# Expert stage of a hybrid decoder layer: weights stationary and tokens moving, in blocks of three tiles with four widths

## What is computed

```python
def routed_experts(h, w_router, b_router, w_up, b_up, w_down, b_down):
    ht = h.reshape(T, D)                                   # 2048 x 1024
    logits = (ht @ w_router + b_router).astype(jnp.float32)
    top_vals, top_idx = lax.top_k(logits, TOP_K)           # 4 of 32
    gate = jax.nn.softmax(top_vals, axis=-1)
    ...
    xs = ht[tok]                                           # 8192 rows, sorted by expert
    hid = lax.ragged_dot(xs, w_up, group_sizes) + b_up[e_sorted]       # 1024 -> 2048
    x_glu = jnp.minimum(hid[:, 0::2], SWIGLU_LIMIT)
    x_lin = jnp.clip(hid[:, 1::2], -SWIGLU_LIMIT, SWIGLU_LIMIT)
    act = x_glu * jax.nn.sigmoid(SWIGLU_ALPHA * x_glu) * (x_lin + 1.0)
    out = lax.ragged_dot(act, w_down, group_sizes) + b_down[e_sorted]  # 1024 -> 1024
    out = out * gate.reshape(-1)[order][:, None].astype(out.dtype)
    y = jnp.zeros_like(ht).at[tok].add(out)
```

## Time and profile before

| | |
|---|---|
| median of 3 runs | 5605.09 us (5603.74 to 5606.45) |
| profiled execution, its span | 5600.4 us |
| TensorE products busy | 5200.6 us, 93% |
| weight loads busy | 4371.7 us, 78% |
| VectorE, ScalarE, GpSimd busy | 49%, 35%, 12% |
| bytes moved by DMA | 810.15 MB, mean 145 GB/s |

### The profile page before, as it was taken

How to read it: one execution, slowest core, us unless ns; L and a number is a source line. 1 busy time by engine, 2 the same in 40 slices (tenths; PEclk the granted TensorE clock), 3 DMA queues, 4 the chain that set the end, 5 groups by cost and what they waited for, 6 DMA issues and landing times.

```text
span 5600.4 us, 88876 instructions
## 1 busy us (share of the span) xinstructions
PE 5200.6 (93%) x24906; PEld 4371.7 (78%) x24907; DVE 2741.4 (49%) x5402; ACT 1934.0 (35%) x3754; POOL 679.8 (12%) x767
## 2 busy tenths in 40 slices
PE   7999999998687799896999999999999999999996
PEld 6888888887566678685887878778877787888885
DVE  3000000000699744354566565775666666665564
ACT  3111111111355522222344444553444434343333
POOL 0000000000344300022011111111111111110110
PEclk7999999999799899897999999999999999999998
DMA  3221222122223243443467465764666656554556
GB/s 112 75 75 59 75 75 73 61 75 79 109 99 120 99 170 136 159 142 117 151 191 231 154 195 164 232 223 157 196 208 190 216 169 192 158 170 154 162 167 196
DMA packets 387048, 810.15 MB, mean 145 GB/s; under 512 B 62259, under 2 KB 113715, under 8 KB 380724
## 3 DMA queue, kind: packets, MB, share of 16 engines
q1 hardware_dynamic: 361188, 722.92, 37.5%
q0 software_dynamic: 25808, 86.59, 6.7%
HBM read 662.47 MB, written 155.26 MB: 146 GB/s over the span
## 4 chain that ended last, share of the span: by engine, by line
PE 46%; DMA 2%; DVE 2%; issue 1%; ACT 1%; DVEq 0%; SPq 0%; ACTq 0%; POOL 0%; POOLq 0%
PE e_acc L253 15%; PE e_acc L255 14%; PE e_acc L254 14%; DMA e_raw<-in_w_down 2%; PE e_xT L2049 1%; PE e_aT L2058 1%; DVE e_hid L2009 1%; ACT e_whi L1913 0%; DVE e_wlo L1974 0%; SPq L1806 0%; DVE e_alo L1984 0%; DVE e_glu L2011 0%; DMA e_xg<-h,e_rec_in 0%; ACT e_sg L1948 0%; DVE e_glu L2016 0%
## 5 line engine op out<-in xcount | busy, mean ns | idle before, releaser
L1974 DVE TENSOR_TENSOR e_wlo<-e_raw,e_whi 128x512 fp32r<-128x512 f32 x1544 | 953.1, 687 | 210.5 <-ACT e_whi L1913 207.7
L253 PE MATMUL e_acc<-e_whi,e_xhi 128*128 128x512 f32 x2592 | 1031.7, 398 | 17.8 <-issue 15.0
L255 PE MATMUL e_acc<-e_whi,e_xlo 128*128 128x512 f32 x2592 | 1012.9, 391 | 0.0
L254 PE MATMUL e_acc<-e_wlo,e_xhi 128*128 128x512 f32 x2592 | 1011.7, 390 | 0.0
L1913 ACT CAST e_whi<-e_raw 128x512 fp32r<-128x512 f32 x1544 | 830.9, 619 | 124.7 <-issue 84.7
L253 PE MATMUL p_acc<-p_hi,hT_hi 128*128 128x464 f32 x2048 | 765.8, 374 | 14.2 <-DVE p_lo L348 14.2
L255 PE MATMUL p_acc<-p_hi,hT_lo 128*128 128x464 f32 x2048 | 764.5, 373 | 0.0
L254 PE MATMUL p_acc<-p_lo,hT_hi 128*128 128x464 f32 x2048 | 761.7, 372 | 0.0
L348 DVE TENSOR_TENSOR p_lo<-p_raw,p_hi 128x464 fp32r<-128x464 f32 x128 | 79.5, 642 | 1078.9 <-ACT p_hi L318 1078.4
L253 PEld LDWEIGHTS e_acc<-e_whi,e_xhi 128*128 128x128 f32 x2592 | 487.2, 188 | 125.3 <-issue 27.9
L255 PEld LDWEIGHTS e_acc<-e_whi,e_xlo 128*128 128x128 f32 x2592 | 487.1, 188 | 103.1
(11 more groups left out here) (284 smaller groups left out, 6575.8 us busy)
## 6 DMA issues: line engine op xcount, KB each, us to landing
e_raw<-in_w_up SPq DMA_DIRECT2D x1032, 256.0 KB, 5.1
e_raw<-in_w_down SPq DMA_DIRECT2D x512, 256.0 KB, 6.7
z<-p_z SPq DMA_DIRECT2D x256, 232.0 KB, 2.0
e_bias<-in_b_up SPq DMA_DIRECT2D x129, 256.0 KB, 5.6
p_raw<-in_w_in SPq DMA_DIRECT2D x128, 232.0 KB, 2.8
b_gates<-z SPq DMA_DIRECT2D x16, 1536.0 KB, 7.1
oT<-x_oT SPq DMA_DIRECT2D x16, 1024.0 KB, 3.9
b_raw<-oT SPq DMA_DIRECT2D x16, 1024.0 KB, 9.4
```

Source lines behind the costliest of these rows:

```text
L253: pe.matmul(out, x_hi(k), w_hi(k), start=first, stop=False)
L254: pe.matmul(out, x_hi(k), w_lo(k), start=False, stop=False)
L255: mm = pe.matmul(out, x_lo(k), w_hi(k), start=False, stop=last)
L1974: dve.tensor_tensor(w_lo[s % 2][:, k, :], raw[:, k, :], w_hi[s % 2][:, k, :].bitcast(F32), ALU.subtract).then_inc(lo_made.sem, 1)
```

## The change

The roles of the operands are swapped in `run_experts`. A 128x128 piece of the weights is stationary, and the tokens of one block move: `x_hi` and `x_lo` (then `a_hi`, `a_lo`) hold channels on partitions and up to 384 tokens side by side. A block has at most three tiles. The planner writes into each row of the table which of four widths (256, 288, 320, 384 tokens) covers the tokens of the block, and TensorE branches to one of four copies of its code for the block, with that width in each product. A slice is now four fills (`j`), one for each 128 of its output columns, of 24 products each; the result has channels on partitions and tokens as columns.

The up columns are sorted while they are split: `pairs` reads every second column of `raw`, `banks` writes them side by side, so that a fill gives either clamped-half or linear-half channels. The bias is one number per partition now; all biases are loaded and turned once, at the start, and added as a column operand in the instruction that empties the bank. Activations need no transposes any more; outputs do (`turn_y`), before ScalarE gates them. VectorE now does both clamps, always over 384 columns; GpSimd keeps the indirect DMAs and two small copies. SyncE loads the next records after slice 2's weights instead of slice 1's.

```diff
-BLOCK_TILES = 4
+BLOCK_TILES = 3
+WIDTHS = (256, 288, 320, 384)
...
+            link(dve.tensor_copy(cntf[:], rkp[:, 0:E]))
...
+            link(dve.tensor_scalar(wide[:, 1:2], wide[:, 0:1], float(WIDTHS[0]), None, ALU.is_gt))
+            for w in WIDTHS[1:-1]:
+                link(dve.scalar_tensor_tensor(out=wide[:, 1:2], in0=wide[:, 0:1], scalar=float(w), in1=wide[:, 1:2],
+                                              op0=ALU.is_gt, op1=ALU.add))
...
+        def pairs(w, k, s):
+            if s >= UP:
+                return w[:, k, :]
+            return w[:, k, :].rearrange("p (h n a) -> p h a n", h=Q // 2, a=2)
+        def banks(w, k, s):
+            if s >= UP:
+                return w[:, k, :]
+            return w[:, k, :].rearrange("p (h a n) -> p h a n", h=Q // 2, a=2)
...
         def _(act):
-            def split(b, s, free):
+            def split(b, s, ks):
...
-                    act.copy(w_hi[s % 2][:, k, :], raw[:, k, :]).then_inc(hi_made.sem, 1)
+                    act.copy(banks(w_hi[s % 2], k, s), pairs(raw, k, s)).then_inc(hi_made.sem, 1)
...
+                for s in range(UP):
+                    for h in range(2):
+                        n = 2 * s + h
+                        act.wait_ge(taken.sem, taken.after(b, 2 * n + 1))
+                        act.activation(sg[n % 2][:], glu[n % 2][:], ACT.Sigmoid, scale=ALPHA).then_inc(sg_made.sem, 1)
+                        split(b, s + 1, range(4 * h, 4 * h + 4))
+                        act.wait_ge(av_made.sem, av_made.after(b, n + 1))
+                        act.copy(a_hi[:, n, :], av[n % 2][:]).then_inc(a_hi_made.sem, 1)
...
         def _(dve):
...
+            def open_glu(b, n):
+                dve.wait_ge(summed.sem, summed.after(b, 2 * n + 1))
+                dve.tensor_scalar(glu[n % 2][:], acc[2 * n % Q][:, 0:CAP], bias_now[:, n:n + 1], LIMIT, ALU.add,
+                                  ALU.min).then_inc(taken.sem, 1)
+            def open_lin(b, n):
+                dve.wait_ge(summed.sem, summed.after(b, 2 * n + 2))
+                dve.tensor_scalar(lin[n % 2][:], acc[(2 * n + 1) % Q][:, 0:CAP],
+                                  bias_now[:, CHUNKS + n:CHUNKS + n + 1], LIMIT + 1.0, ALU.add,
+                                  ALU.min).then_inc(taken.sem, 1)
+            def finish_down(b, s, j):
+                dve.wait_ge(summed.sem, summed.after(b, s * Q + j + 1))
+                n = 2 * CHUNKS + (s - UP) * Q + j
+                dve.tensor_scalar(yT[s % 2][:, j, :], acc[j][:, 0:CAP], bias_now[:, n:n + 1], None,
+                                  ALU.add).then_inc(taken.sem, 1)
...
                 for s in range(UP):
+                    for h in range(2):
+                        n = 2 * s + h
+                        open_glu(b, n)
+                        if n > 0:
+                            split_a(b, n - 1)
+                        dve.wait_ge(sg_made.sem, sg_made.after(b, n + 1))
+                        dve.tensor_tensor(glu[n % 2][:], glu[n % 2][:], sg[n % 2][:], ALU.mult).then_inc(gl_made.sem, 1)
+                        split(b, s + 1, range(4 * h, 4 * h + 2))
+                        open_lin(b, n)
+                        dve.wait_ge(gl_made.sem, gl_made.after(b, n + 1))
+                        dve.wait_ge(taken.sem, taken.after(b, 2 * n + 2))
+                        dve.scalar_tensor_tensor(out=av[n % 2][:], in0=lin[n % 2][:], scalar=1.0 - LIMIT,
+                                                 in1=glu[n % 2][:], op0=ALU.max, op1=ALU.mult).then_inc(av_made.sem, 1)
+                        split(b, s + 1, range(4 * h + 2, 4 * h + 4))
+                split_a(b, CHUNKS - 1)
...
+                finish_down(b, UP, 2)
+                split(b, UP + 1, range(6, 8))
+                finish_down(b, UP, 3)
+                for j in range(Q):
+                    split(b + 1, 0, range(2 * j, 2 * j + 2))
+                    finish_down(b, UP + 1, j)
...
         def _(pe):
+            def fill(b, s, j, width, hi, lo, halved=None):
+                pe.wait_ge(taken.sem, taken.after(b, s * Q + j - Q + 1))
+                cols = slice(j * P, (j + 1) * P)
                 for k in range(KD):
...
+                    pe.matmul(acc[j][:, 0:width], w_hi[s % 2][:, k, cols], hi[:, k, 0:width], start=k == 0, stop=False)
+                    pe.matmul(acc[j][:, 0:width], w_lo[s % 2][:, k, cols], hi[:, k, 0:width], start=False, stop=False)
+                    mm = pe.matmul(acc[j][:, 0:width], w_hi[s % 2][:, k, cols], lo[:, k, 0:width], start=False,
+                                   stop=k == KD - 1)
+                mm.then_inc(summed.sem, 1)
+            def expert(b, before, now, following, width):
+                for s in range(UP):
+                    pe.wait_ge(lo_made.sem, lo_made.after(b, (s + 1) * KD))
+                    if s == 0:
+                        pe.wait_ge(x_lo_made.sem, now.prior + now.live + 1)
+                    for j in range(Q):
+                        fill(b, s, j, width, x_hi, x_lo)
+                        if s == 0 and j == 1:
+                            turn_y(before, UP + 1, 0, taken.after(b, 0))
+                            turn_y(before, UP + 1, 1, taken.after(b, 0))
+                        if s == 0 and j == 3:
+                            turn_y(before, UP + 1, 2, taken.after(b, 0))
+                turn_x(following, 0)
+                pe.wait_ge(lo_made.sem, lo_made.after(b, (UP + 1) * KD))
+                for j in range(Q):
+                    fill(b, UP, j, width, a_hi, a_lo, a_lo_made if j == 0 else None)
+                    if j < 2:
+                        turn_x(following, j + 1)
+                pe.wait_ge(lo_made.sem, lo_made.after(b, (UP + 2) * KD))
+                for j in range(Q):
+                    fill(b, UP + 1, j, width, a_hi, a_lo)
+                    if j == 0:
+                        turn_y(now, UP, 0, taken.after(b, (UP + 1) * Q))
+                        turn_y(now, UP, 1, taken.after(b, (UP + 1) * Q))
+                    if j == 1:
+                        turn_y(now, UP, 2, taken.after(b, (UP + 1) * Q))
```

More of the change, by code:

```diff
@@ L1860, in scatter @@
                 with block.tile(i):
-                    pool.wait_ge(y_gated.sem, block.down(SLICES - 1, i) + 1)
+                    pool.wait_ge(y_gated.sem, block.out(SLICES - 1, i) + 2)
                     pool.wait_ge(y_sent.sem, (block.prior + i) * 16)
@@ L1934, in _ @@
+            summed.open(act)
+            y_gated.open(act)
             act.preload_act_table(ACT.Sigmoid)
-            split(0, 0, (up_summed.sem, 0))
+            split(0, 0, range(KD))
             first = Block(act, 1)
             for i in first.each():
-                split_x(first, i, 0)
+                split_x(first, i, summed.after(0, 0))
             with act.Fori(0, count(act)) as b:
-                now = Block(act, b + 1)
+                before, now = Block(act, b), Block(act, b + 1)
@@ L1963, in _ @@
-                split(b + 1, 0, (down_summed.sem, now.down(UP + 1, 0)))
-                for i in now.each():
-                    gate(now, UP + 1, i)
+                        split_x(following, i, summed.after(b, UP * Q))
+                    if i < 2:
+                        split(b, UP + 1, range(4 * i, 4 * i + 4))
+                split(b + 1, 0, range(4))
+                with now.tile(0):
+                    gate(now, UP, 0)
+                with now.tile(1):
+                    gate(now, UP, 1)
@@ L1967, in _, with split @@
+                split(b + 1, 0, range(4, KD))
+                with now.tile(2):
+                    gate(now, UP, 2)
+            last = Block(act, count(act))
+            for i in last.each():
+                gate(last, UP + 1, i)
         @blk.vector
         def _(dve):
-            lo_made.open(dve)
-            def split(b, s):
-                for k in range(KD):
+            def split(b, s, ks):
+                for k in ks:
                     dve.wait_ge(hi_made.sem, hi_made.after(b, s * KD + k + 1))
-                    dve.tensor_tensor(w_lo[s % 2][:, k, :], raw[:, k, :], w_hi[s % 2][:, k, :].bitcast(F32),
-                                      ALU.subtract).then_inc(lo_made.sem, 1)
+                    dve.tensor_tensor(banks(w_lo[s % 2], k, s), pairs(raw, k, s),
+                                      banks(w_hi[s % 2], k, s).bitcast(F32), ALU.subtract).then_inc(lo_made.sem, 1)
@@ new lines, in _ @@
+            lo_made.open(dve)
+            x_lo_made.open(dve)
+            for n in range(Q):
+                dve.memset(acc[n][:], 0.0).then_inc(cleared.sem, 1)
+            dve.wait_ge(cleared.sem, Q)
+            taken.open(dve)
+            dve.wait_ge(bias_turned.sem, 1)
+            for i in range(ROWS):
+                es = slice(i * E // ROWS, (i + 1) * E // ROWS)
+                for a in range(3):
+                    at = (3 * i + a) * P
+                    dve.tensor_scalar(bias[:, es, a * CHUNKS:(a + 1) * CHUNKS],
```

(37 more changed lines are left out.)

306 lines of the change are left out of this document (117 added, 189 removed).

## The result

The changed kernel takes 6243.18 us, the median of four runs (6235.51 to 6261.39). The kernel before took 5605.77 us beside it. The ratio is 1.1143, 95% interval [1.1125, 1.1162]: slower by 637 us. The forecast was 5683 us, with a range of 5500 to 5975; the sign was right, the size far off, and the time lies outside the range.

What follows compares the result with a forecast made beforehand. The prediction took TensorE's own stream in the expert stage as the bound: 2373 products + 106 transposes + 384 pauses + 15 issue + 96 clock = 2974 us against 2902, with 6 outside +78, so 5683 us; range 5500 to 5975.

Steps and rivals of the forecast that it cites:

- The products: TensorE's expert-stage products: 18432 at 120, 133.3 and 146.7 ns for 256, 288 and 320 columns, 2373 us, 271 us fewer.
- A fixed 13.3 ns: Cost of each TensorE product beyond its column stream at 2.4 GHz, taken from 512-column products as equal for every width.
- rivals 1: Expert-stage product costs follow columns plus weight columns, 136 ns at 256 columns: +275 us, 5958 us; chance 0.18.
- 2 (112 ns): At 256 columns only the weight load's 112 ns remains and pauses spare the clock: 2197 us of products, 5411 us; chance 0.23.
- The formula that the forecast took from the Trainium skill: Spacing of TensorE products as columns over 2.4 GHz plus 2.5 ns: 2172 us of products, not used for the term.
- The transposes and small waits: TensorE transposes left on the path, 24 per two-tile block and 36 per three-tile block: 972, 106 us, 35 fewer.
- The pauses: TensorE waits after slices 0 to 3 for VectorE's tail from open_lin to the last splits: 128 of 3.0 us, 384 us.
- The clock: Granted clock falls to half after pauses: two dips a block, 64 of 1.5 us each, 96 us, between 0 and 192.
- the forecast's own signs of being wrong: Products at 112 or 136 ns, pauses under 2 us, clock 1.00 throughout or below 0.9, e_wlo waits within down slices.
- rival 3: VectorE becomes the bound in up slices because splits reading every second weight cost 0.53 us more: +310 us, 5990 us; chance 0.07.
- the 15.0 of issue stay: TensorE's issue waits in the expert stage carried over unchanged from the kernel before: 15 us.
- its lower bound of 2197 us: Least total for the expert-stage products, with widths of 256, 288 and 320 columns at 112, 123 and 136 ns.

Runs made afterwards that it cites:

- one320: The changed kernel with one copy of TensorE's block code, always 320 columns wide, instead of a choice by width: 6071.54 us.
- two: The changed kernel with two copies of TensorE's block code, 288 and 320 columns, instead of four: 6198.11 us.
- dead: one320 with a second copy of the same code in front of the used one, behind a branch never taken: 6332.57 us.
- rolled_two: The changed kernel with the next slice's splits moved earlier, two copies (256 and 320 columns), and each copy's four up slices rolled into a two-pass loop: 5582.52 us.
- paired_three: The changed kernel with earlier splits, three copies (256, 288, 320 columns), all six slices one three-pass loop, operand addresses from registers: 5671.89 us.
- four320: The changed kernel with its four copies and branches kept, but every copy 320 columns wide: 6512.88 us.
- lean_two: rolled_two with TensorE's register loads at a block's start cut from seven to three, the others read where used: 5446.15 us.

## Why the prediction was wrong

**The products: right.** Starts lie 119, 132 and 147 ns apart at 256, 288 and 320 columns; 120, 133 and 147 were forecast. The timeline at 288 and at 320 columns:

```profile
2866.80 0.29 PE L2113 MATMUL e_acc<-e_ahi,e_whi 128*128 128x288 f32 x1
...
2867.86 0.29 PE L2115 MATMUL e_acc<-e_alo,e_whi 128*128 128x288 f32 x1
...
4106.05 0.31 PE L2115 MATMUL e_acc<-e_xlo,e_whi 128*128 128x320 f32 x1
...
4106.93 0.31 PE L2115 MATMUL e_acc<-e_xlo,e_whi 128*128 128x320 f32 x1
```

From 2866.80 to 2867.86 eight distances are 1.06 us, 132.5 ns each; from 4106.05 to 4106.93 six are 0.88 us, 147 ns each. A fixed 13.3 ns beside the stream holds down to 256 columns. With that rivals 1 (136 ns at 256 columns) and 2 (112 ns) fall.

The formula that the forecast took from the Trainium skill (TensorE: Matmul & The Clock Gate, section Back-to-back issue gap) has 109 ns at 256 columns, an estimate. The section gives it for a product by itself and says that for a stream of products with a load each it counts too little at few columns. The trace agrees with the latter: 119 ns.

**The transposes and small waits: right.** 106 us forecast, 102 measured.

**The pauses: right.** 384 us forecast, 377 measured, and the chain is the one that was worked out term by term. All of one pause in the timeline:

```profile
3008.03 0.28 PE L2115 MATMUL e_acc<-e_xlo,e_whi 128*128 128x256 f32 x1
3008.44 0.61 DVE L2011 TENSOR_SCALAR e_lin<-e_acc,e_bias_now 128x384 f32<-128x384 f32 x1
3009.16 0.56 DVE L2059 SCALAR_TENSOR_TENSOR e_av<-e_lin,e_glu 128x384 f32<-128x384 f32 x1
3009.63 1.29 DVE L1989 TENSOR_TENSOR e_wlo<-e_raw,e_whi 128x512 fp32r<-128x512 f32 x2
3011.05 0.38 PE L2113 MATMUL e_acc<-e_xhi,e_whi 128*128 128x256 f32 x1 [2.74 <-DVE e_wlo L1989]
```

`open_lin` 0.61, the activation product 0.56, two splits 1.29, as forecast within 0.08. That the down slices have none is right too: all 128 waits on e_wlo stand after slices 0 to 3.

**The clock: near at the pauses, without the rest.** 96 us stood for 64 dips of 3.4 us. The stage has 72 dips of that length, and about 114 us are lost behind pauses. That is luck in part: two dips a block were taken as the middle between none and four, not worked out. Another 65 us are lost behind the block starts, whose gaps the sum didn't have. The granted clock of 0.89 in the stage is one of the forecast's own signs of being wrong (below 0.9).

**VectorE as the bound (rival 3): fell.** VectorE is busy for 1912.6 us of the stage, 54% and not the 70% that were forecast, and the groups of VectorE show that a split of every second element costs what it cost before:

```profile
L1989 DVE TENSOR_TENSOR e_wlo<-e_raw,e_whi 128x512 fp32r<-128x512 f32 x1544 | 994.2, 685 | 2.5
```

**The step that failed: "the 15.0 of issue stay".** The part on the change priced products, transposes, splits and waits, and carried the issue row over from the kernel before as if the stream of instructions cost nothing to deliver. The diff turned the loop's body into four copies of a whole block behind two branches. That is a new resource, and neither a term nor a rival stood for it, not even with a bound. In the place of 15 us stand 481, and with the clock behind them 546. That is 531 more than the forecast had, of the 556 us by which the stage missed. Without these the changed kernel would be near 5710 us, an estimate (6243 less 531), still slower than the kernel before: the sign was forecast rightly, but five sixths of the 637 us come from what the forecast did not have. The step has two parts. Most of the time is branches that wait for code. The rest is the register loads at a block's start, seven now where the kernel before had four. There they hid behind products that still ran, in one320 three of the six did, and behind a long branch all seven show. The trace of before had a hint that nobody priced: a row for instruction packets on its page, 26 packets, which is a loop that runs without loading code. With the four copies it is 367.

Three smaller slips of the forecast change no chance: its lower bound of 2197 us is 2202 with the terms as it gives them, the 2172 us by the page's formula are 2173, and the sign turns at an extra of 9.1 ns (13.3 less 78 us over 18432 products), not 8.5.

The Trainium skill has what was needed (Runtime: NRT & Kernel Launch, section Instruction fetch mechanics): TensorE's instruction memory holds 2048 instructions, it is refilled in blocks of 16 KiB, and a taken branch to code that isn't held waits for a DMA. The long branches of the trace, 3.3 to 5.8 us each, agree with the last. Whole copies agree with the bound: one of 1248 instructions or more loads nothing after its first pass, two (two, dead) and four load in every pass, and so do three rolled ones (2592) in most. rolled_two, with 1728 or more, is near it and loads at seven starts of 31. paired_three, with 1440 or more, loads all the same; its amount alone doesn't explain that. The section also says that only two blocks are held. That does not agree with one320: it goes round a loop of at least 1248 instructions, nearly five blocks, and loads nothing in it (25 packets in the whole run).

**The account of the changed kernel, by runs.** Taking away the extra copies gained 172 us although it gave up 270 us of narrower products; so the copies cost 441 (four320 less one320). Taking away the pauses gained 406. Both together, with 256 columns kept for the small blocks and fewer register loads at a block's start, gave 5446 us, 797 less than the changed kernel.

## What to carry to other kernels

Count the instructions between the two ends of a loop on each engine, with the branches that are jumped over, when a change writes copies of its body; if the copies are many, every pass may load its code anew, and the page's row for instruction packets shows it. Split first what hangs on the last result of a stage, and put register loads where products are queued ahead of them. A gap that is long enough for the granted clock to fall costs more than itself: in the changed kernel 377 us of pauses brought 114 us of clock with them, and 481 us of block starts 65.

## What the hardware showed that was not expected

- Code is loaded in packets of 16 KB on a queue of its own, and TensorE waits for it in its branches: 85 of them took 3.3 to 5.8 us in the stage of the changed kernel, where the others took 0.07 to 0.25. A loop of one copy runs with no load after its first pass; with two unrolled copies or more in it, run or not, each pass loads and waits 7 to 19 us where it jumps. Loads within a copy, where the code runs straight on, cost nothing that the trace shows (four320 against one320).
- Code that is never run counts: one dead copy cost 261 us.
- A load of one word into a register of TensorE takes 0.30 us, and the next follows some 0.77 us behind it. A block start with seven of them and no code load takes 4.4 to 4.9 us from product to product (rolled_two), one with three 1.3 to 1.7 (lean_two). The list of waits names this only "issue"; the rows of the loads' own line show it.
- Behind one copy code is loaded anew and behind its neighbour it isn't, with no difference in use (22 us behind a block of 256 columns, 6 us behind one of 288, in paired_three). This was not explained.
